# Expert rows gathered into two buffers a side instead of three at the start of an encoder kernel's retrieval stage

## The chip, the cores and the metric

The kernel runs on one core of a Trainium2 chip. The metric is the device time of one execution in microseconds (us); less is better.

## The reference, cut to what matters

One encoder layer over 512 tokens of width 2048. After a mixing stage (`w_out`, norm ln1) and a cross-attention into 256 memory tokens (norm ln2), a retrieval FFN picks for each token, by product keys, 16 experts in each of 8 heads, 128 in all, and sums them:

```python
x = layer_norm(DN_ALPHA * x + y_mem, ln2_g[l], ln2_b[l])      # the second norm
...
u_sel = jnp.take(peer_u, ib, axis=0)
act = jax.nn.gelu(jnp.einsum('thkd,td->thk', u_sel, xb), approximate=False) * gb
v_sel = jnp.take(peer_v, ib, axis=0)
return jnp.einsum('thk,thkd->td', act, v_sel)
```

`peer_u` and `peer_v` are 16384 x 2048 in f32.

## The kernel before, in words

The 512 tokens are four blocks of 128 (b0 to b3). For blocks b2 and b3 the experts are done **densely**, on TensorE (all experts streamed through, with gates that are zero for those not chosen). For blocks b0 and b1 they are done by **rows**: row r of a block is the r-th chosen expert of each of its 128 tokens, and there are 256 rows, 128 a block. For each row GpSimd (POOL) issues an indirect DMA that gathers one row of `peer_u` for each token (128 x 2048 f32, 1.05 MB; `u_row`, L719) and one of `peer_v` (`v_row`, L734). VectorE (DVE) multiplies the first with the tokens and sums (`dot`, L2280), ScalarE applies the gelu to four sums at a time, and DVE adds the second, scaled, to the accumulator (`add_row`, L2291). In the row stage DVE goes `dot(k+4)`, `add(k)`, `dot(k+5)`, `add(k+1)` and so on.

A gather goes into a row buffer, and `buffer_turns` (L248) lays out by hand which: each buffer is open in one or more intervals of r, and each row takes the open buffer used longest ago. u has two buffers open all the time, a third (index 3) in rows 0 to 15 (`EARLY`, L244), and another third (index 2) from row 26 on. v is alike: two always, index 4 in rows 0 to 15, index 3 from row 22 on. The buffers of `EARLY` lie on GAIN_G and GAIN_B, the places that hold the second norm's two vectors (ln2_g, ln2_b) copied to all partitions. A `u_row` or `v_row` first waits (L714, L725) until DVE has used the row that lay in its buffer before. POOL issues in one fixed order: u0 u1 u2 u3, then u4 v0 u5 v1 u6 v2 and so on, so a gather that waits holds all behind it.

GAIN_G and GAIN_B are first needed by the second norm of b0 (`b0.x2`, L2381), and again by that of b2 and b3 (L2425) and of b1 (L2435). As rows 0 to 15 overwrite them, POOL loads them a second time after the gather of v18 (L744 to L748, two loads of 1.05 MB), and DVE waits for that at L2424 (`gain2_in`).

All of this runs beside TensorE (PE), whose weights SyncE (SP) streams through four slots of 1.05 MB. In the stretch concerned DVE's order is written out by hand (L2383 to L2435): `best_keys`/`best_pairs` (top-16 search), then rows in small groups by `some_rows(n)`, mixed with what PE needs: `add_mix` (L2184) adds PE's product of `w_out` to x, `first_norm` (L1843 to L1849) is norm ln1 of a block. In order: rows 0-3, add_mix of column part 2, rows 4-7, add_mix of part 3, norm of b2, rows 8-9, add_mix of part 0, rows 10-13, add_mix of part 1 (named mix31.1), norm of b3 (ln1_3), norm of b1 (ln1_1), best_keys(2), best_pairs(0, 2), rows 14-15, then the softmax maxima of b2 and b3 (L2201).

PE's order at the same place (L1217 to L1229): the products of `w_out` (L1022), then `b_pq(0, 2)` (L1048), then the transposes of b2 (L1040, waits for ln1_2), of a query tile, and of b3 (`told` at L1112: waits for ln1_3), then `d_features` (L1124).

Of the kernel before, what the change touches and what calls it, by code (L numbers as in the profile page):

```python
# [33 lines left out]
P = 128  # L34
D = 2048
# [117 lines left out]
RSTEPS = 2 * HK // 4  # L153
# [84 lines left out]
DVE_AT = {n: k + 1 for k, n in enumerate(DVE_STEPS)}  # L238
# [2 lines left out]
GELU_AT = [16 * k for k in range(1, 4)]  # L241
U2_FROM = 2 * HALVES_BEFORE + 6
V2_FROM = 2 * HALVES_BEFORE + 30
EARLY = (0, 16)  # L244
MORE_U, MORE_V = (26, 2 * HALVES_BEFORE - 22), (22, 2 * HALVES_BEFORE - 26)


def buffer_turns(times):  # L248

    last, turns = {}, []  # L250
    for r in range(4 * RSTEPS):
        open_now = [e for e in range(len(times)) if any(a <= r < b for a, b in times[e])]
        e = min(open_now, key=lambda k: last.get(k, -1))
        turns.append((e, last.get(e)))
        last[e] = r
    return turns


ALWAYS = (0, 4 * RSTEPS)
U_TURNS = buffer_turns([[ALWAYS], [ALWAYS], [MORE_U, (U2_FROM, 4 * RSTEPS)], [EARLY]])  # L260
V_TURNS = buffer_turns([[ALWAYS], [ALWAYS], [(V2_FROM, 4 * RSTEPS)], [MORE_V], [EARLY]])
U2_LATE = min(r for r in range(U2_FROM, 4 * RSTEPS) if U_TURNS[r][0] == 2)
U_MORE_LAST = max(r for r in range(U2_FROM) if U_TURNS[r][0] == 2)
V_MORE_LAST = max(r for r in range(V2_FROM) if V_TURNS[r][0] == 3)
# [25 lines left out]
def build(nc, x, memT, pos, cols_d, w_once, w_mix, w_row, w_feat, wq_pairs, lru_w, keysT, gains, peer_u, peer_v,  # L290
          peer_ut, peer_vt, gates_d, x0_d, out):
    N_ONCE = w_once.shape[0]
    with ExitStack() as ctx:
        def sem(name):
            return ctx.enter_context(nc.semaphore(name))
# [5 lines left out]
        def place(name, cols, at=None, dt=F32):  # L301
            at = at0[0] if at is None else at
            at0[0] = at + cols
            assert at + cols <= ARENA, (name, at + cols)
            v = arena[:, at:at + cols]
            return v if dt == F32 else v.bitcast(dt)
# [13 lines left out]
        GAIN_G, GAIN_B = C[:, 0:D], C[:, D:2 * D]  # L320
        SC, SC2, MISC = 38912, 43008, 51712
# [15 lines left out]
        for n in (I_, H_):  # L337
# [16 lines left out]
        assert at0[0] <= MISC  # L354


        UB = [place("u0", D, 8192), place("u1", D, 10240), place("u2", D, SC2),
              GAIN_G]
        VB = [place("v0", D, 12288), place("v1", D, 16384), place("v2", D, SC2 + 2 * D),
              place("v3", D, SC2 + D), GAIN_B]  # L360
        ACC = place("acc", D, 14336)
        ACC1 = X[:, 0:D]
        XTD = place("xT dense", DB * D, 18432)
# [76 lines left out]
        def xrow(b):  # L440
            return X[:, b * D:(b + 1) * D]
# [10 lines left out]
        gain0_in, gain1_in, gain2_in, gain3_in = (sem(f"gain{k}_in") for k in range(4))  # L452
# [26 lines left out]
        wb_full = [sem(f"wb_full{s}") for s in range(SLOTS)]  # L479
        wb_used = sem("wb_used")  # L480
        steps_mm, steps_ev, steps_dv = sem("steps_mm"), sem("steps_ev"), sem("steps_dv")
        u_full = [sem(f"u_full{e}") for e in range(4)]
        v_full = [sem(f"v_full{e}") for e in range(5)]
        u_free, v_free = sem("u_free"), sem("v_free")
        gel_done, act_done = sem("gel_done"), sem("act_done")
        sk_free, idx_ready, top_done, gate_exp, gated = (sem(n) for n in ("sk_free", "idx_ready", "top_done", "gate_exp", "gated"))
# [163 lines left out]
        @block.gpsimd  # L650
        def _(pool):
            pool.memset(IDENT, 0.0).then_inc(consts_set, 1)
            pool.memset(ONES, 1.0).then_inc(consts_set, 1)
            for e in range(2):
                pool.memset(LX[e], 0.0).then_inc(consts_set, 1)
            pool.iota(IOTA, pattern=[[1, NK]], base=0, channel_multiplier=0,
                      allow_small_or_imprecise_dtypes=True).then_inc(consts_set, 1)
            pool.wait_ge(consts_set, 5)
            pool.affine_select(out=IDENT, in_=IDENT, compare_op=ALU.not_equal, fill=1.0, base=0,
                               pattern=[[-1, P]], channel_multiplier=1).then_inc(consts2_set, 1)  # L660

            for n in range(2):
                pool.dma_start(LWT[n], lru_w[n]).then_inc(lw_full[n], 16)
            for b in range(NB):
                pool.wait_ge(ln0_done, b + 1)
                pool.dma_start(x0_d[b * P:(b + 1) * P, :], xrow(b)).then_inc(x0_out[b], 16)
            for n in range(2, NL):
                pool.wait_ge(r_mm, n - 1)
                pool.dma_start(LWT[n % 2], lru_w[n]).then_inc(lw_full[n % 2], 16)

            def x0_again(b):
                pool.wait_ge(x0_out[b], 16)
                pool.dma_start(xrow(b), x0_d[b * P:(b + 1) * P, :]).then_inc(x0_back[b], 16)

            pool.wait_ge(product_mm, made(QUADS - 1, "p3"))
            x0_again(0)
            pool.wait_ge(lru_done, NL + 1)

            def load_queries(hp, part):
                cols = slice(part * 512, (part + 1) * 512)  # L680
                pool.dma_start(WQ[:, cols], wq_pairs[hp][:, cols]).then_inc(wq_full[part], 16)

            for part in (2, 0, 1):
                load_queries(0, part)
            for hp in range(1, PAIRS):
                pool.wait_ge(qpe_mm, hp)
                load_queries(hp, 2)
                pool.wait_ge(qn_mm, 2 * hp - 1)
                load_queries(hp, 0)
                pool.wait_ge(qn_mm, 2 * hp)  # L690
                load_queries(hp, 1)
                x0_again(hp)
            pool.wait_ge(qn_mm, HEADS)
            pool.dma_start(GAIN_G, gains[4:5, :].partition_broadcast(P)).then_inc(gain2_in, 16)
            pool.dma_start(GAIN_B, gains[5:6, :].partition_broadcast(P)).then_inc(gain2_in, 16)
            pool.wait_ge(pv_mm, HEADS)
            pool.dma_start(GAIN1_G, gains[2:3, :].partition_broadcast(P)).then_inc(gain1_in, 16)
            pool.dma_start(GAIN1_B, gains[3:4, :].partition_broadcast(P)).then_inc(gain1_in, 16)


            def load_gates(q):
                pool.wait_ge(g_ready, q - 1)
                pool.dma_start(WD[q % 2].rearrange("p (g n) -> p g n", g=DT // TG),
                               gates_d[:, :, q * 8 * TG:(q + 1) * 8 * TG].rearrange("g p n -> p g n")
                               ).then_inc(wd_in_late[q % 2], 16)

            def u_row(r):
                e, before = U_TURNS[r]
                if r % 32 == 0:
                    pool.wait_ge(idx_ready, r // 32 + 1)  # L710
                if r == U2_LATE:
                    pool.wait_ge(gates_out, 16 * (DT // TG))
                elif before is not None:
                    pool.wait_ge(u_free, before + 1)  # L714
                elif e == 2:
                    pool.wait_ge(steps_mm, PE_AT["d.pv"])
                elif e == 3:
                    pool.wait_ge(steps_dv, DVE_AT["b0.x2"])
                pool.indirect_dma_start(UB[e], None, peer_u, bass.IndirectOffsetOnAxis(ap=IDX[:, r:r + 1], axis=0)  # L719
                                        ).then_inc(u_full[e], 16)  # L720

            def v_row(r):
                e, before = V_TURNS[r]
                if before is not None:
                    pool.wait_ge(v_free, before + 1)  # L725
                elif e == 1:
                    pool.wait_ge(wb_used, W_AT["mix0.1.3"])
                elif e == 2:
                    pool.wait_ge(sk_free, 16)
                elif e == 3:  # L730
                    pool.wait_ge(steps_mm, PE_AT["d.pv"])
                elif e == 4:
                    pool.wait_ge(steps_dv, DVE_AT["b0.x2"])
                pool.indirect_dma_start(VB[e], None, peer_v, bass.IndirectOffsetOnAxis(ap=IDX[:, r:r + 1], axis=0)  # L734
                                        ).then_inc(v_full[e], 16)

            for s in range(4):
                u_row(s)
            for j in range(RSTEPS):
                for s in range(4):  # L740
                    if j + 1 < RSTEPS:
                        u_row(4 * j + 4 + s)
                    v_row(4 * j + s)
                    if 4 * j + s == EARLY[1] + 2:  # L744
                        pool.wait_ge(u_free, EARLY[1])
                        pool.wait_ge(v_free, EARLY[1])
                        pool.dma_start(GAIN_G, gains[4:5, :].partition_broadcast(P)).then_inc(gain2_in, 16)
                        pool.dma_start(GAIN_B, gains[5:6, :].partition_broadcast(P)).then_inc(gain2_in, 16)  # L748
                    for q in range(4, NK // 8):
                        if GATES_AFTER[q] == 4 * j + s:  # L750
                            load_gates(q)
# [1063 lines left out]
        def _(dve):  # L1815
# [603 lines left out]
            for c in QUAD:  # L2419
                for tb in range(DB):  # L2420
                    add_memory(2 + tb, c, (c % 2) * 2 + tb, f"d.wo{c}", f"d.wo{c}.{tb}")
                if c == 0:
                    best_pairs(0, 3)
            dve.wait_ge(gain2_in, 64)  # L2424
            layer_norm(2, "d.wo3.0", GAIN_G, GAIN_B, "d.x2_0")  # L2425
            layer_norm(3, "d.wo3.1", GAIN_G, GAIN_B, "d.x2_1")
            some_rows(2)
# [181 lines left out]
```

## Time and profile before

| | |
|---|---|
| median of 3 runs | 3091.31 us (3091.04 to 3093.08) |
| the profiled execution, its own time | 3092.15 us |
| its span, first to last instruction | 3090.3 us |
| mean granted TensorE clock | 0.994 of full speed |
| PE busy | 3019.6 us, 98% |
| DVE busy | 2141.1 us, 69% |
| POOL busy | 708.7 us, 23% |
| indirect gathers | 256 of u and 256 of v |

Busy time is the sum of an engine's instructions. In rows of the timeline the first number is the start in us from the span's start, the second the duration, and a bracket at the end tells how long the engine stood idle before and what released it. "x36" is the number of instructions merged in the row; an f32 matmul of 512 columns counts as two.

### The profile page before, as it was taken

Reading aid. Unit: us, or ns where it says so; the run is one execution under the profiler, and the core shown is the slowest. Engines: PE = TensorE matmul, PEld = TensorE weight load, DVE = VectorE, ACT = ScalarE, POOL = GpSimd, SP = SyncE. Lnnn points to the kernel's source line nnn. Section 1 sums busy time; section 2 is a strip of 40 time slices with the busy share of each in tenths; the row PEclk is TensorE's granted clock in tenths of the full one; section 3 lists DMA queues with packets and bytes.
Section 4 is the critical chain, followed back from the end, with each engine's and each line's share of the span. In section 5 each row is a group of like instructions: output and inputs, shape, how many; then the busy total and the mean of one; then the engine's idle time right before and its main releaser. Section 6 shows DMA issues by size and latency. Waiting matters only on the chain.

```text
span 3090.3 us, 27875 instructions
## 1 busy us (share of the span) xinstructions
PE 3019.6 (98%) x10918; PEld 1982.3 (64%) x10918; DVE 2141.1 (69%) x3110; ACT 365.6 (12%) x682; POOL 708.7 (23%) x568
## 2 busy tenths in 40 slices
PE   8999999999999999999999997999999999999998
PEld 5888854444455786798874445884458874468743
DVE  6567875524887799999987767656566665656676
ACT  1322223301002211122200000000000000000000
POOL 0000000000421434322133433322222232222330
PEclk9999999999999999999999998999999999999999
DMA  8222222377988999999999999999999999999996
GB/s 339 75 89 89 82 99 78 136 258 259 391 342 309 381 362 397 417 367 389 373 388 407 388 422 421 419 418 416 421 421 422 418 418 416 421 421 422 406 421 239
DMA packets 152867, 1032.00 MB, mean 334 GB/s; under 512 B 16672, under 2 KB 20896, under 8 KB 36000
## 3 DMA queue, kind: packets, MB, share of 16 engines
q0 software_dynamic: 80608, 569.41, 45.0%
q1 hardware_dynamic: 72128, 460.81, 38.0%
q8 instruction: 86, 1.41, 0.2%
q14 instruction: 45, 0.37, 0.0%
HBM read 1004.99 MB, written 25.17 MB: 333 GB/s over the span
## 4 chain that ended last, share of the span: by engine, by line
PE 73%; DVE 13%; DMA 10%; issue 2%; ACT 1%; POOL 1%; DVEq 0%; SPq 0%; ACTq 0%; POOLq 0%
PE ps L1273 21%; PE ps L1300 19%; PE ps L819 9%; DMA arena<-peer_v,arena 8%; PE ps L1022 6%; PE ps L1048 3%; DVE arena L2291 3%; PE ps L1124 2%; DVE arena L2332 2%; PE ps L916 1%; DVE arena L2280 1%; DVE arena L2329 1%; PE ps L1159 1%; PE ps L926 1%; PE ps L1316 1%
## 5 line engine op out<-in xcount | busy, mean ns | idle before, releaser
L1273 PE MATMUL ps<-arena 128*128 128x256 f32 x4096 | 896.6, 380 | 23.6 <-ACT arena L1664 22.4
L1273 PEld LDWEIGHTS ps<-arena 128*128 128x128 f32 x4096 | 777.9, 191 | 132.1 <-ACT arena L1664 22.8
L1300 PE MATMUL ps<-arena 128*128 128x512 f32 x1984 | 852.1, 592 | 0.0
L2291 DVE SCALAR_TENSOR_TENSOR arena<-arena 128x2048 f32<-128x2048 f32 x256 | 601.5, 2350 | 290.5 <-DMA arena<-peer_v,arena 217.1
L2280 DVE CUSTOM_DVE_ANT_0 arena<-arena 128x2048 f32<-128x2048 f32 x256 | 585.8, 2289 | 263.2 <-DMA arena<-peer_u,arena 261.0
L1300 PEld LDWEIGHTS ps<-arena 128*128 128x128 f32 x1984 | 377.0, 190 | 472.8 <-issue 472.6
L719 POOL DMA_INDIRECT arena<-peer_u,arena x256 | 353.1, 1379 | 1045.4 <-DVE arena L2280 861.5
L734 POOL DMA_INDIRECT arena<-peer_v,arena x256 | 323.7, 1264 | 700.2 <-DVE arena L2291 674.5
L819 PE MATMUL ps<-arena 128*128 128x256 f32 x1344 | 291.8, 379 | 0.0
L819 PEld LDWEIGHTS ps<-arena 128*128 128x128 f32 x1344 | 255.3, 190 | 39.3 <-issue 5.1
L1364 ACT ACTIVATE arena<-ps 128x512 f32<-128x512 f32 (+3 forms) x285 | 152.6, 571 | 835.3 <-PE ps L1040 114.2
L1022 PE MATMUL ps<-arena 128*128 128x512 f32 x512 | 221.2, 592 | 0.0
L1022 PEld LDWEIGHTS ps<-arena 128*128 128x128 f32 x512 | 97.0, 190 | 120.1 <-issue 120.1
L1646 ACT ACTIVATE arena<-arena 128x4 f32<-128x4 f32 x64 | 13.1, 205 | 1278.5 <-DVE arena L2280 1278.5
L1048 PE MATMUL ps<-arena 128*128 128x512 f32 x320 | 139.4, 593 | 2.5 <-ACT arena L1364 2.5
L1124 PE MATMUL ps<-arena 128*128 128x256 f32 x640 | 139.4, 380 | 1.4 <-ACT arena L1364 1.1
L1124 PEld LDWEIGHTS ps<-arena 128*128 128x128 f32 x640 | 121.1, 190 | 18.9 <-ACT arena L1364 1.5
L1048 PEld LDWEIGHTS ps<-arena 128*128 128x128 f32 x320 | 60.4, 190 | 75.4 <-issue 70.8
L2215 DVE MAX8 arena<-arena 128x8 f32<-128x128 f32 (+1 forms) x192 | 51.9, 326 | 34.8 <-ACT arena L1364 29.2
L1664 ACT ACTIVATE arena<-ps 128x512 f32<-128x512 f32 x64 | 37.6, 593 | 297.1 <-PE ps L1273 296.9
L2332 DVE TENSOR_SCALAR arena<-arena 128x128 f32<-128x128 f32 x256 | 70.7, 342 | 0.0
L1285 PE MATMUL ps<-arena 128*128 128x128 f32 x512 | 68.3, 280 | 0.3
(210 smaller groups left out, 1871.7 us busy)
## 6 DMA issues: line engine op xcount, KB each, us to landing
arena<-peer_ut SPq DMA_DIRECT2D x128, 1024.0 KB, 9.2
arena<-peer_vt SPq DMA_DIRECT2D x128, 1024.0 KB, 9.1
arena<-w_row SPq DMA_DIRECT2D x52, 1024.0 KB, 8.1
arena<-w_mix SPq DMA_DIRECT2D x40, 1024.0 KB, 4.9
arena<-w_once SPq DMA_DIRECT2D x73, 512.0 KB, 5.9
arena<-w_feat SPq DMA_DIRECT2D x20, 1024.0 KB, 9.2
dense_gates<-arena SPq DMA_DIRECT2D x8, 2048.0 KB, 8.1
arena<-dense_gates POOLq DMA_DIRECT2D x12, 1024.0 KB, 24.2
```

The lines of the kernel that those rows point to most:

```text
L719: pool.indirect_dma_start(UB[e], None, peer_u, bass.IndirectOffsetOnAxis(ap=IDX[:, r:r + 1], axis=0)).then_inc(u_full[e], 16)
L734: pool.indirect_dma_start(VB[e], None, peer_v, bass.IndirectOffsetOnAxis(ap=IDX[:, r:r + 1], axis=0)).then_inc(v_full[e], 16)
L819: last = pe.matmul(bank(to, HALF), weights[:, k * P:(k + 1) * P], tokens[:, k, :], start=(fresh and k == 0), stop=(k == KT // 2 - 1), skip ...
L1022: last = pe.matmul(bank(k), Y[:, b * D + kt * P:b * D + (kt + 1) * P], w[:, i * 512:(i + 1) * 512], start=(kt == NL), stop=(kt == NL - 1))
L1048: last = pe.matmul(bank(k), XT[:, kt * P:(kt + 1) * P], w[:, i * 512:(i + 1) * 512], start=(kt == 0), stop=(kt == KT - 1))
L1124: last = pe.matmul(ps[:, k + f // 2, (f % 2) * DT:(f % 2 + 1) * DT], w[:, kt * P:(kt + 1) * P], XTD[:, kt * DT:(kt + 1) * DT], start=(kt = ...
L1273: last = pe.matmul(ps[:, (e // 2) % 4, (e % 2) * DT:(e % 2 + 1) * DT], w[:, kt * P:(kt + 1) * P], XTD[:, kt * DT:(kt + 1) * DT], start=(kt ...
L1300: last = pe.matmul(bank(4 + (c % 2) * 2 + tb), G[:, t * DT + tb * P:t * DT + (tb + 1) * P], w[:, i * 512:(i + 1) * 512], start=(t == 0), s ...
L1364: return act.activation(dst, src, ACT.Copy)
L2280: dve.tensor_tensor_reduce(UB[e], UB[e], xrow(b), 1.0, 0.0, ALU.mult, ALU.add, DOT[r // 4 % 2][:, r % 4:r % 4 + 1]).then_inc(u_free, 1)
L2291: dve.scalar_tensor_tensor(out=acc, in0=VB[e], scalar=AV[r // 4 % 2][:, r % 4:r % 4 + 1], in1=acc, op0=ALU.mult, op1=ALU.add).then_inc(v_f ...
L2332: last = dve.tensor_scalar(oh[:, 0, i], IOTA, turn[:, 0, 4 * n + i:4 * n + i + 1], turn[:, 2, 4 * n + i:4 * n + i + 1], ALU.is_equal, ALU. ...
```

## The change

The intervals `EARLY` go, so rows 0 to 15 use the two buffers that are always open on each side. The second load of the second norm's vectors goes with them, and DVE's wait for it.

```diff
-EARLY = (0, 16)
-U_TURNS = buffer_turns([[ALWAYS], [ALWAYS], [MORE_U, (U2_FROM, 4 * RSTEPS)], [EARLY]])
-V_TURNS = buffer_turns([[ALWAYS], [ALWAYS], [(V2_FROM, 4 * RSTEPS)], [MORE_V], [EARLY]])
+U_TURNS = buffer_turns([[ALWAYS], [ALWAYS], [MORE_U, (U2_FROM, 4 * RSTEPS)]])
+V_TURNS = buffer_turns([[ALWAYS], [ALWAYS], [(V2_FROM, 4 * RSTEPS)], [MORE_V]])
...
-        UB = [place("u0", D, 8192), place("u1", D, 10240), place("u2", D, SC2),
-              GAIN_G]
+        UB = [place("u0", D, 8192), place("u1", D, 10240), place("u2", D, SC2)]
         VB = [place("v0", D, 12288), place("v1", D, 16384), place("v2", D, SC2 + 2 * D),
-              place("v3", D, SC2 + D), GAIN_B]
+              place("v3", D, SC2 + D)]
...
-        u_full = [sem(f"u_full{e}") for e in range(4)]
-        v_full = [sem(f"v_full{e}") for e in range(5)]
+        u_full = [sem(f"u_full{e}") for e in range(3)]
+        v_full = [sem(f"v_full{e}") for e in range(4)]
...
-                elif e == 3:
-                    pool.wait_ge(steps_dv, DVE_AT["b0.x2"])
...
-                elif e == 4:
-                    pool.wait_ge(steps_dv, DVE_AT["b0.x2"])
...
-                    if 4 * j + s == EARLY[1] + 2:
-                        pool.wait_ge(u_free, EARLY[1])
-                        pool.wait_ge(v_free, EARLY[1])
-                        pool.dma_start(GAIN_G, gains[4:5, :].partition_broadcast(P)).then_inc(gain2_in, 16)
-                        pool.dma_start(GAIN_B, gains[5:6, :].partition_broadcast(P)).then_inc(gain2_in, 16)
...
-            dve.wait_ge(gain2_in, 64)
             layer_norm(2, "d.wo3.0", GAIN_G, GAIN_B, "d.x2_0")
```

From row 17 on each row waits for the row two or three before it exactly as it did; only the two always-open buffers swap names.

## Rows read from the trace of the kernel before

**Rows 1.** The page: busy time by engine

```profile
PE 3019.6 (98%) x10918; PEld 1982.3 (64%) x10918; DVE 2141.1 (69%) x3110; ACT 365.6 (12%) x682; POOL 708.7 (23%) x568
```

**Rows 2.** Waits of PE, 560 to 1240 us, then 1240 us on (total, times, longest)

```profile
PE ps L1040 <- ACT arena L1364: 6.7, 4, 4.7
...
PE ps L1273 <- ACT arena L1664: 22.4, 1, 22.4
```

**Rows 3.** Timeline of DVE, dot(2), dot(6), add_mix part 3, dot(17), add(13), mix31.1, ln1_3

```profile
783.42 2.28 DVE L2280 CUSTOM_DVE_ANT_0 arena<-arena 128x2048 f32<-128x2048 f32 x1
...
801.68 2.36 DVE L2280 CUSTOM_DVE_ANT_0 arena<-arena 128x2048 f32<-128x2048 f32 x1 [1.79 <-DMA arena<-peer_u,arena]
...
840.16 1.87 DVE L2184 SCALAR_TENSOR_TENSOR arena<-arena,ps 128x512 f32<-128x512 f32 x3
...
881.63 2.29 DVE L2280 CUSTOM_DVE_ANT_0 arena<-arena 128x2048 f32<-128x2048 f32 x1 [1.94 <-DMA arena<-peer_u,arena]
...
884.74 2.35 DVE L2291 SCALAR_TENSOR_TENSOR arena<-arena 128x2048 f32<-128x2048 f32 x1 [0.80 <-DMA arena<-peer_v,arena]
887.93 1.28 DVE L2184 SCALAR_TENSOR_TENSOR arena<-arena,ps 128x512 f32<-128x512 f32 x2 [0.84 <-PE ps L1022]
...
896.85 2.35 DVE L1849 SCALAR_TENSOR_TENSOR arena<-arena 128x2048 f32<-128x2048 f32 x1
```

**Rows 4.** Timeline of PE, 887 to 907 us

```profile
887.73 13.90 PE L1048 MATMUL ps<-arena 128*128 128x512 f32 x32
901.46 4.09 PE L1040 MATMUL ps<-arena 128*128 128x128 f32 x36
905.39 1.06 PE L1107 MATMUL ps<-arena 128*128 128x128 f32 x8
```

**Rows 5.** Busy time by stretch (PE, PEld, DVE, ACT, POOL; PEclk; DMA share; GB/s)

```profile
800.00:888.00 88.00, 88.00 (x206) 38.95 (x205) 69.36 (x64) 0.61 (x3) 39.11 (x25) 1.00 1.01 422
888.00:928.00 40.00, 39.73 (x175) 29.34 (x174) 36.61 (x99) 5.50 (x11) 0.00 (x0) 1.00 0.65 259
```

**Rows 6.** Timeline of POOL: the gathers u4 and u5

```profile
774.14 0.94 POOL L719 DMA_INDIRECT arena<-peer_u,arena  x1 [0.30 <-issue]
...
785.98 2.74 POOL L719 DMA_INDIRECT arena<-peer_u,arena  x1 [9.67 <-DVE arena L2280]
```

**Rows 7.** L719, issue to landing: u0; u9 to u14 (804 to 842 us); u20

```profile
DMA to landing us min/median/max: 5.6/5.6/5.6
...
DMA to landing us min/median/max: 16.5/18.0/18.9
...
DMA to landing us min/median/max: 7.5/7.5/7.5
```

**Rows 8.** Timeline of POOL: the gathers v9, u14 and u15

```profile
834.93 2.97 POOL L734 DMA_INDIRECT arena<-peer_v,arena  x1 [3.15 <-DVE arena L2291]
838.20 2.86 POOL L719 DMA_INDIRECT arena<-peer_u,arena  x1 [0.30 <-issue]
...
854.22 2.81 POOL L719 DMA_INDIRECT arena<-peer_u,arena  x1 [11.92 <-DVE arena L2280]
```

**Rows 9.** L734, three gathers of v, 1639 to 1656 us: issue to landing

```profile
DMA to landing us min/median/max: 12.6/13.2/13.8
```

**Rows 10.** Timeline of PE: after its wait of 4.7 us, and the same work later

```profile
1204.40 8.48 PE L1273 MATMUL ps<-arena 128*128 128x256 f32 x32
...
1241.60 7.07 PE L1273 MATMUL ps<-arena 128*128 128x256 f32 x32
```

**Rows 11.** Timeline of DVE: first maximum after rows 14-15, then mix of b2/b3

```profile
939.81 1.23 DVE L2201 TENSOR_REDUCE arena<-ps 128x4 f32<-128x1024 f32 x1 [5.05 <-PE ps L1132]
...
987.80 1.28 DVE L2190 SCALAR_TENSOR_TENSOR arena<-arena,ps 128x512 f32<-128x512 f32 x2 [5.58 <-PE ps L1159]
```

**Rows 12.** Second load of the vectors, its second half: issue on POOL, and issue to landing

```profile
954.62 0.60 POOL L748 DMA_DIRECT2D arena<-gains  x1
...
DMA to landing us min/median/max: 14.9/14.9/14.9
```

## The prediction

> **What bounds the kernel now.** I read the page first: PE is busy 98% of the span [rows 1], so the time is PE's work plus its waits, and a change on DVE, POOL or the DMAs counts only where it alters a wait of PE. Next the waits of PE by stretch [rows 2]: from 560 to 1240 us no wait is longer than 4.7 us, and after that one counts, 22.4 us on a gelu of ACT that stands behind late rows, near 1900 us. So most handovers between PE and DVE are nearly tied, and the question is how much room DVE has in rows 0 to 15.
>
> The timeline of DVE shows it. add(13) starts at 884.74 and lasts 2.27 up to the next start, so DVE is free at 887.01; mix31.1 starts at 887.93 after 0.84 us of waiting **for PE**, and ln1_3 ends at 896.85 + 2.35 = 899.2 [rows 3]. PE needs ln1_3 for the transposes of b3. It begins 36 transposes at 901.46 and the next product at 905.39, 0.109 us each; 20 come before those of b3, so PE asks at 903.6 [rows 4]. DVE's room before add(13) is late enough to hurt is 0.9 + (903.6 - 899.2) = **5.3 us**.
>
> What paces DVE there are the gathers, not its own work. dot(6) at 801.68 and dot(17) at 881.63 both waited for their gather [rows 3]: 11 rows in 79.95 us, 7.27 us a row, 3.64 us a gather. The DMA engines are full over just this stretch, at 422 GB/s from 800 to 888 us, and at 259 GB/s in the 40 us after it [rows 5]. Where the queue is full, what is put off is not made up.
>
> **The change, part by part.**
>
> *Start.* Before, u4 went out at 774.14, with v0 right behind, while DVE searched for best pairs [rows 6]. With two buffers u4 must wait for dot(2), which starts at 783.42 [rows 3] and ends 2.2 later, 785.6; v0 stands behind it on POOL. So u4 and v0 take the places in the queue that u5 (785.98, [rows 6]) and v1 had, and each later gather that of the one a row before. One row's pace: **+7.3 us**. u2 and u3 have no such cost: u2 now goes out after dot(0), some 12 us before dot(2) asks, and a gather on a nearly idle queue lands in 5.6 to 7.5 us [rows 7].
>
> *The norm of b2.* Before, u14 was issued at 838.20 and v10 right after, ahead of the norm, and u14 landed up to 18.9 us later, so the queue never emptied; u15 went out at 854.22, when dot(12) behind the norm was done [rows 7, 8]. With two buffers u14 itself must wait for dot(12). That ends at about 854 + 7.3 = 861.2, and u14 lands 7.5 us later [rows 7], at 868.7. The last gather issued before the norm is v9, which was issued at 834.93 and at up to 18.9 us to landing was there by 853.8 [rows 7, 8]; now it lands near 861.1. The gap is 7.6 us in place of 3.64: **+4.0 us**.
>
> *Pace elsewhere.* With two buffers four gathers are out at most. At 18 us from issue to landing [rows 7] that would not do, but this time is the queue's depth, six gathers of 3.64 us less what DVE holds; with four it falls. The nearest rows are those of v near 1640 us, where v has two buffers and u three: 12.6 to 13.8 us [rows 9]. 13.2 plus the add's 2.3 is 15.5 us for two rows, 7.75 a row, where 7.27 holds now: at worst 0.5 x 10 rows = 5 us, at best nothing, since PE took weights faster there. I take 0, as each gap in the queue beyond the norm's seems covered.
>
> *Sum for add(13):* 7.3 + 4.0 = **11.3 us late**. Less the room of 5.3, PE waits **6.0 us** for ln1_3, near 904 us. add_mix of part 3 is late too: it began at 840.16 and took 1.9 [rows 3], so it now ends near 850, and PE wants its banks only for `b_pq(0, 2)` at 887.73 [rows 4]; part 2 has as much room. That costs nothing.
>
> *The clock.* Behind the 4.7 us wait near 1200 us [rows 2] 32 matmuls took 8.48 us where they take 7.07 [rows 10]: 1.4 us lost to the lower of the clock's two levels, 1.2 GHz, and the transposes just before them were slow too. I add **1.6 us**.
>
> *Is it passed on?* DVE comes to the maxima of b2 and b3 with 5.05 us to spare [rows 11]. It is now 10.4 us late (11.3 less 0.9), PE 7.6; 2.8 is less than 5.05, so DVE again waits for PE, and so it does at 987.80 [rows 11]. From there both run 7.6 us late with the same distances between them. The gathers from row 17 on wait as before, and the weight slots are full in the quiet stretch [rows 5]. Nothing in the row stage near 1600 to 1918 us starts by a clock of its own: it begins when PE's and DVE's one-hot stage ends, so the 22.4 us wait [rows 2] moves along and stays.
>
> *What goes away.* Two loads of 1.05 MB, 5 us of DMA time at 422 GB/s. The second was issued at 954.62 and landed 14.9 later, 969.5 [rows 12]; DVE comes to the wait at L2424 after 987.80 [rows 11], so it was long met. POOL saves 2 x 0.6 us of issuing while DVE is busy with other work than rows. The longest waits of PE there [rows 2] name no DMA. 0 taken; as bounds 0, and -1.2 for POOL.
>
> Against the profiled execution: span 3090.3 + 7.6 = 3097.9, own time 3092.15 + 7.6 = 3099.8; that execution lies 0.8 above the median, so the median comes to 3091.3 + 7.6 = **3099 us**.
>
> *Row and rule.* A single gather takes 5.6 us on an idle queue and 16.5 to 18.9 us in the stretch concerned [rows 7], against 6.75 us that two buffers cover (an add, a dot and an add between dot(r) and dot(r+2)). The Trainium skill, "DMA: Bandwidth & Descriptors", section on the anatomy of one DMA on the SWDGE path, gives 2.0 us plus bytes over 436 GB/s for one transfer, estimated 4.4 us here. By that two buffers would hide each gather, and the time would stay 3091.3. The trace disagrees for this stretch, though not for u0; that outcome is the first rival, with its 0.08.
>
> **Rivals.**
>
> *It stays hidden (not slower).* The mechanism: u4 and v0 start late into a queue that was at less than full rate before 800 us, so part of their 7.3 us is made up there, and the gap at the norm is covered by DVE's own delay. If add(13) comes less than 5.3 us late, PE sees nothing: 3091.3. It decides at ln1_3 against 903.6. Against it: the start alone costs 7.3, and the DMA engines are full from 800 on [rows 5].
>
> *Depth decides.* If gathers keep taking 18 us with four of them out, two rows cost 18 + 2.3 and a row 10.15 us: 2.9 more for each of some 12 rows, 35 us, less 10 for what the norm lets land, plus 7.3. add(13) is 32 late, PE waits 27 us: about 3120. Against it [rows 9].
>
> *Made up later.* The PE wait of 22.4 us near 1900 us takes in the loss: then 3091.3. Or the two loads' 5 us of DMA time and POOL's 1.2 us come off the end as well, 3091.3 - 6.2 = 3085. Against it: that wait hangs on the row chain, which starts late too, and nothing waited for the loads [rows 12].
>
> **How the numbers follow.** About 0.2% (6.2 us) is what a measurement of this kernel can tell from no change, and the forecast lies just above it. Case one (a wait of PE before b3's transposes), 0.80: with the start's 7.3 alone it gives a wait of 2.0 and 3093.3; with 5 us of pace 11.0 plus 1.8 and 3104.1. Of its 0.80 I put 0.56 above 3097.5 and 0.24 below. Hidden 0.08, depth 0.06, made up later 0.06 (0.04 within, 0.02 below). Slower 0.56 + 0.06 = 0.62; same 0.24 + 0.08 + 0.04 = 0.36; faster 0.02. The range takes in the hidden case and case one's ends with 2 us for what I can't size: 3091 to 3106; outside are most of the depth case and single us at the lower side.
>
> **What would show it.** Right: u4 issued near 786 us instead of 774; dot and add each about one row later from 800 us on; the first landing after the norm of b2 some 7.5 us after dot(12); add(13) near 896; a new wait of PE at L1040 on DVE L1849 of about 6 us near 904 us with a lower granted clock behind it; DVE's wait before L2201 down from 5.05 to about 2; the same 22 us near 1905. Wrong: no wait of PE at 904 us; a landing time still near 18 us with two buffers; a wait at 904 us with the end of the span unmoved.

## The result, and the profile after

| | before | changed |
|---|---|---|
| median | 3091.45 us (8 runs, 3088.23 to 3093.08) | 3101.91 us (8 runs, 3096.84 to 3104.45) |
| ratio | | 1.0033, 95% interval 1.0024 to 1.0042 |
| span of the profiled execution | 3090.3 us | 3101.0 us |

The change costs 10.5 us at the medians, 10.7 at the spans. The forecast was 3099 us, between 3091 and 3106, and slower with a chance of 0.62. A single execution of a kernel here lies up to 7 us off that kernel's median, so below each step is read from the trace, and the medians only back it.

In the changed kernel's listing the code behind L741 has line numbers smaller by 11: add_row is L2280 (was L2291), dot L2269 (L2280), the end of a norm L1838 (L1849), PE's transposes L1029 (L1040), add_mix L2173 (L2184); `u_row` is L715 and `v_row` L728.

The page of the changed kernel, span and busy time. PE's busy time is up by 2.3 us [rows 1], though its instructions are the same: some ran at the lower clock.

```profile
span 3101.0 us, 27871 instructions
...
PE 3021.9 (97%) x10918; PEld 1983.9 (64%) x10918; DVE 2142.0 (69%) x3110; ACT 365.3 (12%) x682; POOL 687.4 (22%) x566
```

The waits of PE in the changed kernel, 560 to 1240 us and from 1240 us on (total, times, longest). The first line was 0.5 us in all before (longest 0.2), and the fourth is new; the second and the last answer to [rows 2]; the third, on the adds of b1's memory product, was 3.6 us before too. The last has moved with everything else and is not spent.

```profile
PE ps L1029 <- DVE arena L1838: 8.1, 3, 7.6
PE ps L1029 <- ACT arena L1353: 5.2, 4, 3.2
PE ps L1162 <- DVE arena L2179: 3.6, 1, 3.6
...
PE ps L1029 <- DVE arena L2173: 1.2, 1, 1.2
...
PE ps L1262 <- ACT arena L1653: 23.3, 1, 23.3
```

The timeline of PE in the changed kernel, 885 to 950 us, answering to [rows 4]. PE waits 1.19 us for mix31.1 and 7.59 for ln1_3. The last line is the score product of b2 and b3 (L1132 before), which began at 937.9 then.

```profile
887.57 13.90 PE L1037 MATMUL ps<-arena 128*128 128x512 f32 x32
902.65 2.40 PE L1029 MATMUL ps<-arena 128*128 128x128 f32 x20 [1.19 <-DVE arena L2173]
912.65 3.67 PE L1029 MATMUL ps<-arena 128*128 128x128 f32 x16 [7.59 <-DVE arena L1838]
916.12 1.30 PE L1096 MATMUL ps<-arena 128*128 128x128 f32 x8
...
948.31 3.62 PE L1121 MATMUL ps<-arena 128*128 128x256 f32 x16
```

The timeline of DVE in the changed kernel, answering to [rows 3, 11]: dot(4), dot(5), add(13), mix31.1, the last instruction of ln1_3, the first maximum, and the last adds of b2's and b3's memory product.

```profile
793.07 2.29 DVE L2269 CUSTOM_DVE_ANT_0 arena<-arena 128x2048 f32<-128x2048 f32 x1 [4.50 <-DMA arena<-peer_u,arena]
...
801.48 2.29 DVE L2269 CUSTOM_DVE_ANT_0 arena<-arena 128x2048 f32<-128x2048 f32 x1 [2.49 <-DMA arena<-peer_u,arena]
...
899.05 2.35 DVE L2280 SCALAR_TENSOR_TENSOR arena<-arena 128x2048 f32<-128x2048 f32 x1 [2.67 <-DMA arena<-peer_v,arena]
901.32 1.28 DVE L2173 SCALAR_TENSOR_TENSOR arena<-arena,ps 128x512 f32<-128x512 f32 x2
...
910.24 2.35 DVE L1838 SCALAR_TENSOR_TENSOR arena<-arena 128x2048 f32<-128x2048 f32 x1
...
950.24 1.22 DVE L2190 TENSOR_REDUCE arena<-ps 128x4 f32<-128x1024 f32 x1 [2.08 <-PE ps L1121]
...
998.23 1.28 DVE L2179 SCALAR_TENSOR_TENSOR arena<-arena,ps 128x512 f32<-128x512 f32 x2 [5.58 <-PE ps L1148]
```

add(13) starts at 899.05 in place of 884.74: 14.3 us late. DVE's wait for PE ahead of the maxima fell from 5.05 to 2.08, and the one at 998.23 is again 5.58: from there both engines run as before, 10.4 us later.

The timeline of POOL in the changed kernel: u4, v9 and u14. Then the times from issue to landing of v9, of u14, and of the seven u gathers issued from 804 to 845 us, answering to [rows 7, 8].

```profile
785.83 2.75 POOL L715 DMA_INDIRECT arena<-peer_u,arena  x1 [10.92 <-DVE arena L2269]
...
847.83 0.94 POOL L728 DMA_INDIRECT arena<-peer_v,arena  x1 [2.53 <-DVE arena L2280]
861.54 2.81 POOL L715 DMA_INDIRECT arena<-peer_u,arena  x1 [12.78 <-DVE arena L2269]
...
DMA to landing us min/median/max: 13.2/13.2/13.2
...
DMA to landing us min/median/max: 7.6/7.6/7.6
...
DMA to landing us min/median/max: 9.8/11.5/12.4
```

v9 lands at 847.83 + 13.2 = 861.0 and u14 at 861.54 + 7.6 = 869.1, a gap of 8.1 us. Busy time of the changed kernel by stretch (PE, PEld, DVE, ACT, POOL; PEclk; DMA share; GB/s), against [rows 5]: the queue is not quite full up to the norm's end, nearly a third empty in the gap, full behind it. The last row is PE's clock just behind its wait.

```profile
800.00:861.00 61.00, 61.00 (x144) 27.02 (x143) 47.84 (x49) 0.41 (x2) 20.80 (x15) 1.00 0.99 414
861.00:869.00 8.00, 8.00 (x20) 3.57 (x19) 8.00 (x8) 0.00 (x0) 6.67 (x3) 1.00 0.89 299
869.00:899.00 30.00, 30.00 (x71) 13.30 (x70) 16.49 (x13) 0.21 (x1) 7.49 (x8) 1.00 1.01 421
...
914.00:918.00 4.00, 4.00 (x23) 3.92 (x22) 3.50 (x13) 2.74 (x5) 0.00 (x0) 0.67 0.44 180
```

### The profile page after: what moved, and what is told of

It is laid out like the page before. It is cut to its first block, busy times and chain, and to the rows that moved or that the text cites. A ratio compares the mean times of both kernels' runs of the same rounds, so it can differ in the third digit from the quotient of the medians.

```text
span 3101.0 us, 27871 instructions
## 1 busy us (share of the span) xinstructions
PE 3021.9 (97%) x10918; PEld 1983.9 (64%) x10918; DVE 2142.0 (69%) x3110; ACT 365.3 (12%) x682; POOL 687.4 (22%) x566
## 4 chain that ended last, share of the span: by engine, by line
PE 63%; DVE 18%; DMA 12%; issue 4%; POOL 1%; ACT 1%; DVEq 0%; SPq 0%; ACTq 0%; POOLq 0%
PE ps L1289 19%; PE ps L1262 18%; DMA arena<-peer_v,arena 11%; PE ps L808 9%; DVE arena L2280 5%; PE ps L1011 2%; DVE arena L2321 2%; DVE arena L2269 2%; PE ps L1037 2%; DVE arena L2207 2%; PE ps L1113 1%; PE ps L905 1%; DVE arena L2204 1%; DVE arena L2318 1%; PE ps L1148 1%
## 5 line engine op out<-in xcount | busy, mean ns | idle before, releaser
L1262 PE MATMUL ps<-arena 128*128 128x256 f32 x4096 | 895.3, 380 | 24.9 <-ACT arena L1653 23.3
L2280 DVE SCALAR_TENSOR_TENSOR arena<-arena 128x2048 f32<-128x2048 f32 x256 | 601.6, 2350 | 299.4 <-DMA arena<-peer_v,arena 229.1
L2269 DVE CUSTOM_DVE_ANT_0 arena<-arena 128x2048 f32<-128x2048 f32 x256 | 585.9, 2289 | 278.3 <-DMA arena<-peer_u,arena 276.0
L715 POOL DMA_INDIRECT arena<-peer_u,arena x256 | 343.5, 1342 | 1049.7 <-DVE arena L2269 865.1
L728 POOL DMA_INDIRECT arena<-peer_v,arena x256 | 313.0, 1223 | 729.8 <-DVE arena L2280 707.9
```

What stands on the lines that cost most here:

```text
L1262: last = pe.matmul(ps[:, (e // 2) % 4, (e % 2) * DT:(e % 2 + 1) * DT], w[:, kt * P:(kt + 1) * P], XTD[:, kt * DT:(kt + 1) * DT], start=(kt ...
L2269: dve.tensor_tensor_reduce(UB[e], UB[e], xrow(b), 1.0, 0.0, ALU.mult, ALU.add, DOT[r // 4 % 2][:, r % 4:r % 4 + 1]).then_inc(u_free, 1)
L2280: dve.scalar_tensor_tensor(out=acc, in0=VB[e], scalar=AV[r // 4 % 2][:, r % 4:r % 4 + 1], in1=acc, op0=ALU.mult, op1=ALU.add).then_inc(v_f ...
```

## The experiments

All ratios are to the kernel before on the same chip, its median 3090.1 to 3090.8 us in the three groups of runs. "Late" is always against the profiled execution of the kernel before.

**The loads put back.**

```diff
 changed kernel
+                    if 4 * j + s == 18:
+                        pool.wait_ge(u_free, 16)
+                        pool.wait_ge(v_free, 16)
+                        pool.dma_start(GAIN_G, ...)
+                        pool.dma_start(GAIN_B, ...)
...
+            dve.wait_ge(gain2_in, 64)
```

> The changed kernel with the second load of the two vectors and DVE's wait for it put back; the rows keep two buffers a side. Theory (the loss is the rows' delay, the loads cost nothing): as the changed kernel, 3102 within 3 us, with add(13) near 899, a wait of PE of 8 to 9 us near 904 and 1.2 us more of issuing on POOL near 965. Rival (the loads' DMA time matters, and their removal gave back part of the loss): 3 to 6 us above the changed kernel.

Measured: 3100.7 us, ratio 1.0036 (1.0022 to 1.0050). add(13) at 898.0, PE waits 7.58 us. Within the scatter of single executions that is the changed kernel. The loads cost nothing that can be seen, and taking them away gave nothing back.

**v0 and v1 first.**

```diff
 changed kernel (the new calls are on one line here)
-            for s in range(4):
-                u_row(s)
+            u_row(0); u_row(1); v_row(0); v_row(1); u_row(2); u_row(3)
...
-                    v_row(4 * j + s)
+                    if 4 * j + s >= 2:
+                        v_row(4 * j + s)
```

> The changed kernel, but POOL issues v0 and v1 right after u1, ahead of u2. Theory (7 us of the loss come from v0 standing behind u4 on POOL, so that two gathers fewer are done when the full stretch begins): add(13) 7 us earlier than in the changed kernel, at 892, PE's wait for ln1_3 1 to 3 us in place of 8.8, and 3093 to 3096. Rival (two buffers make every pair of rows slower, whatever the start): add(13) stays near 899 and the time near 3102.

Measured: 3099.3 us, ratio 1.0028 (1.0017 to 1.0039); add(13) at 896.13, 2.9 us earlier and not 7; PE waits 5.95. The expectation missed, and it was wrong in who stands in whose way. The windows of this kernel show it:

```profile
785.00:800.00 15.00, 15.00 (x36) 6.65 (x35) 10.39 (x14) 3.00 (x4) 7.68 (x4) 1.00 0.63 235
...
800.00:861.00 61.00, 61.00 (x143) 26.98 (x142) 48.36 (x50) 0.41 (x2) 26.71 (x16) 1.00 0.95 393
```

With v ahead the queue runs emptier (235 and 393 GB/s; 284 and 414 in the changed kernel): v2 can't be asked for before add(0), add(0) comes behind dot(4), and dot(4) still waits for u4 until 793.1. v9 lands at 857.0, 3.3 us late instead of 7.3, but u14 comes 10.9 us behind it, so part of the gain is lost again at the norm. The next two runs split the sides.

**The third buffer on one side only.** u alone, then v alone:

```diff
 kernel before
-V_TURNS = buffer_turns([[ALWAYS], [ALWAYS], [(V2_FROM, 4 * RSTEPS)], [MORE_V], [EARLY]])
+V_TURNS = buffer_turns([[ALWAYS], [ALWAYS], [(V2_FROM, 4 * RSTEPS)], [MORE_V]])
```
```diff
 kernel before
-U_TURNS = buffer_turns([[ALWAYS], [ALWAYS], [MORE_U, (U2_FROM, 4 * RSTEPS)], [EARLY]])
+U_TURNS = buffer_turns([[ALWAYS], [ALWAYS], [MORE_U, (U2_FROM, 4 * RSTEPS)]])
```

> The kernel before with the third buffer in rows 0 to 15 on the u side alone; v has two. With v0 and v1 issued early (e2) add(13) came only 2.9 us earlier, so what lags at the start should be u4 waiting for dot(2), and v with it. Theory (the start's term is u's): u4 and v0 go out at 774 as before, add(13) at 886 to 891, PE waits for ln1_3 under 1 us, 3090 to 3093. Rival (both sides count alike, by the number of gathers out): add(13) near 892 and halfway, 3094 to 3097.

> The kernel before with the third buffer in rows 0 to 15 on the v side alone; u has two. Theory (the start's term is u's): nearly as with neither, add(13) at 895 to 899, PE waits 5 to 9 us for ln1_3, 3097 to 3102. Rival (both sides count alike): add(13) near 892, 3094 to 3097.

Measured: u alone 3092.3 us, ratio 1.0002 (0.9992 to 1.0011); v alone 3103.0, ratio 1.0035 (1.0023 to 1.0047). In each kernel's timeline of DVE, add(13) and mix31.1, first u alone:

```profile
890.32 2.35 DVE L2291 SCALAR_TENSOR_TENSOR arena<-arena 128x2048 f32<-128x2048 f32 x1 [2.37 <-DMA arena<-peer_v,arena]
892.58 1.28 DVE L2184 SCALAR_TENSOR_TENSOR arena<-arena,ps 128x512 f32<-128x512 f32 x2
```

then v alone:

```profile
898.47 2.35 DVE L2291 SCALAR_TENSOR_TENSOR arena<-arena 128x2048 f32<-128x2048 f32 x1 [2.68 <-DMA arena<-peer_v,arena]
900.74 1.28 DVE L2184 SCALAR_TENSOR_TENSOR arena<-arena,ps 128x512 f32<-128x512 f32 x2
```

With u alone add(13) is 5.6 us late, just at the edge of DVE's room of 5.3, and PE shows no wait for the norm of b3. With v alone it is 13.7 late, nearly as with neither (14.3), and PE waits 0.61 and 7.58 us. So the third u buffer carries the whole effect on the time. The third v buffer is not worth nothing to DVE: beside the third u buffer it saves those 5.6 us. They don't reach PE only because the room is nearly as large.

**The third buffers in half the rows.**

```diff
 kernel before
-EARLY = (0, 16)
+EARLY = (0, 8)      # and, in the other kernel, (8, 16)
```

In both the second load of the vectors stays where it was, behind v18.

> The kernel before with the extra buffers in rows 0 to 7 alone (EARLY = (0, 8)), so the start and the first full stretch have three buffers a side, the norm of b2 and rows 8 to 13 two. Theory of terms (start 7.2, gap at the norm 4.8, pace behind it 2.3): add(13) some 7 us late, at 892, PE waits 1 to 2 us for ln1_3, 3091 to 3094. Rival (with fewer gathers out the queue is starved all along, and the start is no term of its own): add(13) later than 895.

> The kernel before with the extra buffers in rows 8 to 15 alone (EARLY = (8, 16)): two buffers a side at the start, three across the norm of b2 and behind it. Theory of terms: add(13) some 7 us late from the start alone, less what DVE makes up behind the norm, at 889 to 892; PE waits under 2 us; 3090 to 3094. Rival (the start's delay is made up once three buffers are there, in the norm of b2): add(13) at 885 to 888, and the time of the kernel before.

Measured: rows 0 to 7, add(13) at 891.39 (6.7 late), PE waits 0.83 us, 3092.4 us, ratio 1.0004 (0.9994 to 1.0014). Rows 8 to 15, add(13) at 893.55 (8.8 late), PE waits 3.5 us, 3094.0 us, ratio 1.0011 (1.0001 to 1.0020). The first came as expected. In the second add(13) was some 2 us behind the expected range, and PE waited 3.5 us where under 2 was expected: what the start loses is not made up later even with three buffers. The landings of the gathers (issue plus time to landing) split each delay into its parts:

| kernel | v9 lands | late | v9 to u14 | u14 to v13 | add(13) late |
|---|---|---|---|---|---|
| before | 853.7 | | 3.4 | 27.6 | |
| changed | 861.0 | 7.3 | 8.1 | 29.9 | 14.3 |
| three in rows 0 to 7 | 855.0 | 1.3 | 7.5 | 28.9 | 6.7 |
| three in rows 8 to 15 | 860.9 | 7.2 | 3.1 | 29.6 | 8.8 |
| v alone has three | 861.0 | 7.3 | 8.0 | 29.5 | 13.7 |

The start's delay comes with two buffers at the start, and the wide gap with two buffers at the norm, each without the other. The last stretch, from u14 to v13, is longer than before in all four, even where three buffers serve it. So the two delays add up to 15.5 us, more than the 14.3 with both gone: this part is counted in each. PE's transposes of b3 in the two kernels:

```profile
904.98 1.97 PE L1040 MATMUL ps<-arena 128*128 128x128 f32 x16 [0.83 <-DVE arena L1849]
```
```profile
907.14 3.15 PE L1040 MATMUL ps<-arena 128*128 128x128 f32 x16 [3.50 <-DVE arena L1849]
```

After 0.83 us of waiting they take 1.97 us, after 3.50 they take 3.15. In the second the granted clock from 907.0 to 910.3 us is 0.61 of full speed, in the first it is 1.00 from 905 to 907.

**DVE made late by itself.**

```diff
 kernel before
+            for k in range(22):      # 7 in the other kernel
+                link(dve.bn_stats(STATS[:, 0:6], X[:, 2 * D:2 * D + 512]))
             for k, b in enumerate((3, 1)):
                 add_mix(b, 1, k, "mix31.1")
```

> The kernel before, buffers as they were, with 22 extra small DVE instructions (bn_stats of 512 elements, 14.3 us in all) ahead of mix31.1. Theory (all that matters of the change is that DVE comes to mix31.1 13.4 us late): PE waits 8 to 9 us for ln1_3, the clock costs 1.6, and the time is the changed kernel's, 3100 to 3103. Rival (part of the loss is the gathers' own, later): 3 us or more below the changed kernel.

> The kernel before with 7 of the small DVE instructions ahead of mix31.1 instead of 22 (22 took 16.0 us, so 5.1 us). Theory (DVE has 5.3 us of room there): mix31.1 4.2 us later, no wait of PE for ln1_3 over 0.5 us, and the time of the kernel before, 3089 to 3092. Rival (each us of DVE in this stage is a us of the end): 5 us slower.

Measured: 22 instructions took 16.0 us, not 14.3; 3103.3 us, ratio 1.0043 (1.0026 to 1.0060). 7 of them: 3091.9 us, ratio 1.0001 (0.9991 to 1.0011). The long one, DVE and then PE:

```profile
887.25 15.99 DVE L2406 BATCH_NORM_STATS2 arena<-arena 128x6 f32<-128x512 f32 x22
903.27 1.28 DVE L2184 SCALAR_TENSOR_TENSOR arena<-arena,ps 128x512 f32<-128x512 f32 x2
```
```profile
904.61 2.40 PE L1040 MATMUL ps<-arena 128*128 128x128 f32 x20 [2.74 <-DVE arena L2184]
914.24 3.68 PE L1040 MATMUL ps<-arena 128*128 128x128 f32 x16 [7.23 <-DVE arena L1849]
...
950.69 3.62 PE L1132 MATMUL ps<-arena 128*128 128x256 f32 x16
```

mix31.1 is 15.3 us late and the score product 12.8. In the changed kernel the pair is 13.4 and 10.4: 1.9 and 2.4 us less. With the short delay mix31.1 is at 891.88, 4.0 late, and PE asks for b3's transposes without a wait. Delaying DVE with every gather as before gives the changed kernel's loss, larger by as much as the delay was larger, and below the room it gives none. Nothing else of the change is needed to explain the time.

**The rows put elsewhere.** First behind the norms and best_pairs, then right behind ln1_3:

```diff
 changed kernel
                 add_mix(b, 0, 6 + k, "mix31.0")
-            some_rows(4)
+            some_rows(2)
...
             first_norm(3, "mix3.1")
+            some_rows(2)                # second kernel
             first_norm(1, "mix1.1")
             best_keys(2, "b0.key2")
             best_pairs(0, 2)
-            some_rows(2)
+            some_rows(4)                # first kernel; 2 in the second
```

> The changed kernel, but rows 12 and 13 are worked off behind the norms of b3 and b1 and best_pairs(0, 2), with rows 14 and 15, and not ahead of mix31.1. Theory (the time is lost only where PE waits for ln1_3 behind late rows): no wait of PE on the norm near 904 us; four rows now stand ahead of the maxima of b2 and b3, which come some 4 us late, with 6.8 us of room before PE asks for the probabilities; 3091 to 3094. Rival (late rows cost elsewhere, in the row stage or the DMA queues): 3098 or more.

> The changed kernel with rows 12 and 13 moved to between the norm of b3 (ln1_3) and the norm of b1. Where they stood behind best_pairs, four rows in a run waited 7.9 us for gathers and PE waited 4.7 us for the probabilities. Here their gathers have long landed. Theory: no wait of PE for ln1_3, the maxima of b2 and b3 start near 944 to 946, within the 6.8 us that PE leaves, and 3089 to 3093, the time of the kernel before without its extra buffers. Rival (the late rows cost in the row stage as well): 3097 or more.

Measured, behind best_pairs: 3097.7 us, ratio 1.0026 (1.0015 to 1.0038). The wait for ln1_3 is gone, but another stands in its place. DVE's dot(19) and add(15), the last pair of four rows in a run:

```profile
944.57 2.29 DVE L2269 CUSTOM_DVE_ANT_0 arena<-arena 128x2048 f32<-128x2048 f32 x1 [3.34 <-DMA arena<-peer_u,arena]
...
949.54 2.35 DVE L2280 SCALAR_TENSOR_TENSOR arena<-arena 128x2048 f32<-128x2048 f32 x1 [2.67 <-DMA arena<-peer_v,arena]
```

and PE behind it, waiting for the probabilities:

```profile
956.72 1.97 PE L1129 MATMUL ps<-arena 128*128 128x128 f32 x8 [4.68 <-DVE arena L2197]
```

My expectation had counted DVE's own 4.5 us a row and forgotten that four rows in a run on two buffers wait for their gathers, 7.9 us in all. Measured, behind ln1_3, where the gathers have had the norm's 10 us to land: 3090.5 us, ratio 1.0002 (0.9992 to 1.0011). PE's transposes and DVE's first maximum in that kernel:

```profile
901.30 4.09 PE L1029 MATMUL ps<-arena 128*128 128x128 f32 x36
```
```profile
943.20 1.22 DVE L2190 TENSOR_REDUCE arena<-ps 128x4 f32<-128x1024 f32 x1
```

No wait in either place. Two row buffers a side, no second load, and the time of the kernel before: moving two rows gives back what the buffers gave. That the loss was only undone, and nothing gained beside it, is not shown. The profiled execution was the fastest of ten (3087.5 us), and in it PE's waits of 3.6 us near 1091 and of 4.7 us near 1200 are missing too.

**DVE's idle time filled.** Row 16 ahead of the maxima, row 18 ahead of the last memory add, in the kernel before, and then in the kernel just above:

```diff
             best_pairs(0, 2)
-            some_rows(2)
+            some_rows(3)
...
-            some_rows(2)
+            some_rows(1)
             best_keys(3, "b0.key3")
             for c in QUAD:
+                if c == 3:
+                    some_rows(1)
...
             layer_norm(3, "d.wo3.1", GAIN_G, GAIN_B, "d.x2_1")
-            some_rows(2)
+            some_rows(1)
```

> The kernel before, but DVE works off row 16 ahead of the maxima of b2 and b3, where it waited 5.05 us for PE, and row 18 ahead of the last add of b2's and b3's memory product, where it waited 5.58 us. DVE then has 9 us less to do ahead of the adds of b1's memory product, for which PE waited 3.6 us near 1091 and lost 1.5 to the clock. Theory (DVE's idle time there is worth time): that wait gone, 3085 to 3089. Rival (the rows only wait for gathers elsewhere, or DVE's lead is lost by 1200 us): 3090 to 3092.

> e8_rows_between (two buffers a side, rows 12 and 13 behind ln1_3) with the same two moves as e11_before_gaps. Theory: DVE comes to the maxima 4.5 us later than in e8, past the 6.8 us that PE leaves for the probabilities, so a PE wait of 1 to 4 us near 952; with the wait near 1091 gone it ends at 3088 to 3093. Rival (rows in a run starve on two buffers): 3095 or more.

Measured: on the kernel before 3084.0 us (3082.71 to 3084.29, 8 runs), ratio 0.9976 (0.9966 to 0.9987), the best of all here, faster than both kernels and 1 us below the range expected. Its waits of PE from 560 to 1240 us begin like this; that of 4.7 us [rows 2] and that of 3.6 us on b1's adds are not among them:

```profile
PE ps L1048 <- ACT arena L1364: 2.5, 3, 0.8
PE ps L1040 <- ACT arena L1364: 2.1, 3, 0.7
```

PE is busy 292.2 us of the 300 from 940 to 1240, 284.8 before: 7.4 us more, and the span is 8.1 shorter. On two buffers it gave nothing: 3090.6 us, ratio 0.9998 (0.9989 to 1.0007); DVE now has one row more ahead of the maxima and waits 2.9 us for its gathers, reaches the maxima at 951.80, and PE waits 3.6 us for the probabilities, as the expectation had it.

## Why the prediction was right, and where its sizes were off

*Start, +7.3.* Right in size, measured on v9's landing: 861.0 against 834.93 + 18.8 = 853.7, 7.3 late, and the prediction had it near 861.1. u4 went out at 785.83, as said. The cause is the wait of u4 for dot(2) with v0 behind it: with the third u buffer alone both go out at 774 to 776 us and v9 lands at 854.3, with the third v buffer alone v0 still stands behind u4 and v9 lands at 861.0. v0's place behind u4 is only part of it: v0 and v1 issued early gave back 4.0 of the 7.3.

*Norm of b2, +4.0.* A little small. u14 landed at 869.1 (forecast 868.7), but the gap was 8.1 us where it had been 857.1 - 853.7 = 3.4: 4.7.

*Pace elsewhere, 0 of at most 5.* **This is the term that was mis-sized.** Behind the norm the seven steps from u14's landing to v13's took 29.9 us where they took 27.6: 2.3 us. The landing times fell as argued, from 16.5 to 18.9 us down to 9.8 to 12.4 for u, so "depth decides" fell too. But the 2.3 us are not the price of having fewer gathers out, which is what the prediction's 0 to 5 stood for. The DMA engines moved as much in either kernel over just these seven steps, and with three buffers in rows 8 to 15 the steps took 29.6 us all the same. Busy time by stretch (as in [rows 5]), the kernel before, the changed kernel, and the one with three in rows 8 to 15:

```profile
857.10:884.70 27.60, 27.60 (x65) 12.16 (x64) 20.89 (x17) 0.20 (x1) 10.74 (x8) 1.00 1.01 421
```
```profile
869.10:899.00 29.90, 29.90 (x71) 13.30 (x70) 16.39 (x13) 0.21 (x1) 7.49 (x8) 1.00 1.01 421
```
```profile
864.00:893.60 29.60, 29.60 (x71) 13.10 (x70) 21.01 (x18) 0.20 (x1) 11.06 (x8) 1.00 1.01 421
```

What may take the 2.3 us are the weights. At 421 GB/s there is room beside the seven gathers of 1.05 MB for an estimated 4.3 MB before and 5.2 MB after, one weight load more, which is 2.5 us. SP issues a load every 6.9 us from 840 to 887.8 us and every 3.4 us from there, and the late gathers run into that stretch. No run separates this, so the cause of this term stays open.

*Sum for add(13), 11.3 late.* 14.3. By terms 7.3 + 4.7 + 2.3 = 14.3.

*Room 5.3, wait 6.0.* The room holds: 14.3 - 5.3 = 9.0, and PE waited 1.19 + 7.59 = 8.8. That PE waits for mix31.1 as well, the 1.19, was not foreseen; it adds nothing, as the norm comes behind mix31.1. The two delay kernels measure the room from both sides: 4.0 us late at mix31.1 passes, 15.3 gives 10.0 of waiting.

*Clock, +1.6.* PE's score product is 948.3 - 937.9 = 10.4 us late, of it 8.8 waited, so 1.6 are left, with a granted clock of 0.67 from 914 to 918 us. That it fits so well is partly luck: the slow matmuls cost 2.1, and PE came to the stretch 0.16 us early and lost a wait of 0.27 for ACT. The same remainder is 1.2 us behind the wait of 3.5 and 2.8 behind the two of 2.7 and 7.2.

*Passed on.* Right: the 5.58 us at 998.23, the 23.3 us from 1907 on, and 10.7 us at the end. Nothing downstream took anything in, so "made up later" fell. "It stays hidden" fell with its point, 5.3 us. The rule of the Trainium skill ("DMA: Bandwidth & Descriptors", section on the anatomy of one DMA, 2.0 us plus bytes over 436 GB/s, estimated 4.4 us a gather) would have hidden every gather. The trace disagrees: with four out, from 804 to 845 us, a gather of u takes 9.8 us at the least, against the 6.75 us that two buffers cover.

The miss from 3099 to 3101.9 is these two sizes: 0.7 us at the norm and 2.3 us behind it.

*What goes away, 0.* Right, by the run with the loads kept.

## What to carry to other kernels

Count a buffer by the stage's queue, not by one transfer: with k transfers out in a full queue a landing took up to k times the queue's interval of 3.64 us (here, ahead of the norm, 16.5 to 18.9 us for u with six out, 9.8 to 12.4 with four). Giving up a buffer cost one to two intervals at each place where the next request must now wait for the consumer: 7.3 us at the start and 4.7 behind the long norm. Then look for the first tied handover to the engine that bounds the kernel and compare the delay with its room: 4 us vanished here, and 14 us passed on in full, less the room. Moving two rows past that handover was worth as much as two megabytes of buffers, as long as they did not join a run of rows that waits for its gathers.

## What was not expected of the hardware

A wait of PE of a few us costs more than itself, a very short one does not: 16 transposes took 1.97 us behind a wait of 0.83, 3.15 us behind one of 3.50, and 3.67 behind one of 7.59. A gather's issue on POOL took 0.94 us where DVE stood idle, and up to 2.99 where DVE was in a dot or in the add of a row; with two buffers fewer issues met such work, POOL's busy time fell from 708.7 to 687.4 us, and nothing came of it. And the room for a better order was in the trace of before all along: DVE's two waits for PE of 5.05 and 5.58 us [rows 11], once filled with a row each, gave 6.6 us together.
